# Merge stage of a hybrid attention and mixture-of-experts layer: order of work, early loads, logits from x1, and loads of the first stick-breaking head by columns

## The reference

```
h = rms_norm(x, g1); proj = h @ w_in
ya = banded attention of 8 heads;  yb = stick-breaking attention of 8 heads
gate = sigmoid(gates + b_gate)
merged = gate[0] * (ya @ w_proj_a) + gate[1] * (yb @ w_proj_b)
x = x + merged @ w_out
h2 = rms_norm(x, g2)
x = x + moe(h2)      # top group of 4, top 2 of 8 experts in it, by logits h2 @ [w_group, w_router]
```

## Time and profile before

| what | value |
|---|---|
| three plain runs | 2718.91, 2720.12 (median), 2724.43 us |
| profiled execution, its own time | 2722.95 us |
| its span, first to last instruction | 2721.1 us |
| PE busy, share of the span | 2603.6 us, 96% |
| DVE, ACT, POOL busy | 1634.5, 1491.1, 603.7 us |
| mean granted TensorE clock | 0.976 |
| stick-breaking stage | about 522 to 1290 us |
| merge stage | about 1290 to 1725 us |
| expert stage | about 1726 us to the end |

### The profile page before, as it was taken

One profiled execution on the slowest core, in us unless ns is written; L12 is line 12 of the kernel. 1 busy time (PEld: TensorE's weight loads), 2 busy tenths in 40 slices (PEclk: granted clock), 3 DMA queues, 4 the chain that ended last, 5 costly groups with the idle time before them and its releaser, 6 DMA issues. The chain is left out here.

```text
span 2721.1 us, 41174 instructions
## 1 busy us (share of the span) xinstructions
PE 2603.6 (96%) x13541; PEld 2154.9 (79%) x13542; DVE 1634.5 (60%) x2208; ACT 1491.1 (55%) x2641; POOL 603.7 (22%) x706
## 2 busy tenths in 40 slices
PE   7999999899999999999899999489999999999997
PEld 6788777678888888887799999477788888888886
DVE  4400555388777777776633433588766677766673
ACT  4312776477766676666321211368665577666563
POOL 0000111045444444443000000022211122212111
PEclk9999999999999999999799999699999999999999
DMA  5454444586566556632744433389866788866683
GB/s 174 133 198 150 124 132 129 158 288 211 189 205 190 175 168 188 205 125 99 235 126 132 132 118 96 149 313 390 316 224 228 241 281 313 314 232 223 222 299 64
DMA packets 196351, 536.65 MB, mean 197 GB/s; under 512 B 19928, under 2 KB 70552, under 8 KB 191744
## 3 DMA queue, kind: packets, MB, share of 16 engines
q1 hardware_dynamic: 169616, 432.80, 46.3%
q0 software_dynamic: 26608, 102.17, 13.7%
HBM read 403.36 MB, written 131.53 MB: 197 GB/s over the span
## 5 line engine op out<-in xcount | busy, mean ns | idle before, releaser
L1076 POOL TENSOR_TENSOR sb_sig<-sb_sig,sb_R 128x512 f32<-128x512 f32 (+1 forms) x320 | 340.9, 1065 | 412.9 <-DVE sb_R L1017 412.8
L51 PE MATMUL ex_ps_h<-ex_wu_hi,ex_x_hi 128*128 128x512 f32 x816 | 323.6, 397 | 2.4 <-DVE ex_x_lo L1837 2.4
L53 PE MATMUL ex_ps_h<-ex_wu_hi,ex_x_lo 128*128 128x512 f32 x816 | 319.5, 392 | 0.0
L52 PE MATMUL ex_ps_h<-ex_wu_lo,ex_x_hi 128*128 128x512 f32 x816 | 318.1, 390 | 0.0
L1842 DVE TENSOR_TENSOR ex_wu_lo<-ex_w,ex_wu_hi 128x1024 fp32r<-128x1024 f32 x248 | 285.3, 1217 | 2.5 <-ACT ex_wu_hi L1698 2.0
L1017 DVE TENSOR_TENSOR_SCAN sb_R<-sb_z,sb_R,sb_zeros 128x512 f32<-128x512 f32 x192 | 245.6, 1279 | 56.8 <-ACT sb_z L945 56.4
L1847 DVE TENSOR_TENSOR ex_wd_lo<-ex_w,ex_wd_hi 128x1024 fp32r<-128x1024 f32 x200 | 239.5, 1219 | 52.7 <-ACT ex_wd_hi L1705 52.6
L1698 ACT CAST ex_wu_hi<-ex_w 128x1024 fp32r<-128x1024 f32 x248 | 241.2, 1056 | 11.7 <-DMA ex_w<-in_w_exp 11.7
L957 ACT CAST sb_aT_hi<-sb_pst 128x512 fp32r<-128x512 f32 (+1 forms) x320 | 168.4, 526 | 136.3 <-PE sb_pst L1104 132.9
L1025 DVE TENSOR_TENSOR sb_aT_lo<-sb_pst,sb_aT_hi 128x512 fp32r<-128x512 f32 (+1 forms) x320 | 192.2, 601 | 53.7 <-ACT sb_aT_hi L957 51.0
L944 ACT ACTIVATE sb_sig<-sb_z 128x512 f32<-128x512 f32 (+1 forms) x320 | 172.4, 539 | 82.3 <-PE sb_z L1097 80.9
(11 more groups left out here) (274 smaller groups left out, 6256.5 us busy)
## 6 DMA issues: line engine op xcount, KB each, us to landing
ex_w<-in_w_exp SPq DMA_DIRECT2D x384, 512.0 KB, 8.9
sb_w_hi<-wg_d SPq DMA_DIRECT2D x48, 512.0 KB, 3.6
sb_w_lo<-wg_d SPq DMA_DIRECT2D x48, 512.0 KB, 4.6
gates<-sb_go SPq DMA_DIRECT2D x64, 256.0 KB, 3.8
mo_gates<-gates SPq DMA_DIRECT2D x64, 256.0 KB, 3.7
h<-mo_rows POOLq DMA_DIRECT2D x17, 512.0 KB, 3.0
nt_x<-in_x SPq DMA_DIRECT2D x16, 512.0 KB, 4.6
vhl<-nt_vo SPq DMA_DIRECT2D x16, 512.0 KB, 5.6
```

What stands on the lines that cost most here:

```text
L51: nc.tensor.matmul(out, w_hi, x_hi, start=first, stop=False)
L52: nc.tensor.matmul(out, w_hi, x_lo, start=False, stop=False)
L53: return nc.tensor.matmul(out, w_lo, x_hi, start=False, stop=last)
L1076: nc.gpsimd.tensor_tensor(sig[:, j % 5, 0:width], sig[:, j % 5, 0:width], R[:, r, first:first + width], ALU.mult).then_inc(a_done, 1)
```

## The change

In the stick-breaking stage the first head is loaded in four parts of 512 columns, each with a semaphore of its own, and other loads stand between them; the bias load goes to the end of this list. `round_w` and `split_w` of a piece are placed at step 2 + pc + 2 it at the earliest. In place of the second `wp` tile, SP loads the first chunk of `yaT` into slot 1 of `stage`.

```diff
             load_head(0, slice(0, TC))
-            sp.dma_start(bias[:, :], b_gate).then_inc(bias_in, 16)
-            load_head(0, slice(TC, S))
             load_w(2)
             keep_w(0)
+            load_head(0, slice(TC, 2 * TC))
+            load_w(3)
+            load_head(0, slice(2 * TC, 3 * TC))
             load_v(0)
-            load_w(3)
             keep_w(1)
+            load_head(0, slice(3 * TC, S))
+            sp.dma_start(bias[:, :], b_gate).then_inc(bias_in, 16)
...
-                    for n in range(2):
-                        sp.dma_start(w[:, n, :, :], wp_tiles[n, :, :, :]).then_inc(wp_in[n], 16)
+                    sp.dma_start(w[:, 0, :, :], wp_tiles[0, :, :, :]).then_inc(first_in_next[0], 16)
+                    sp.dma_start(w[:, 1, :, :].rearrange("p k c -> p (k c)").rearrange("p (t s) -> p t s", t=4),
+                                 yaT[:, :, 0:2 * P].rearrange("t p s -> p t s")).then_inc(first_in_next[1], 16)
...
-                        if j == pair_end(it, 2 * pc + 1) + 1:
+                        if j == max(pair_end(it, 2 * pc + 1) + 1, 2 + pc + 2 * it):
                             round_w(it + 2, pc)
...
-                if j % UH == 0 and h or j == 4:
-                    pe.wait_ge(head_in[u], (h // 2 + 1) * 96)
+                if h == g == r == 0:
+                    pe.wait_ge(first_in[ch], 96)
+                if j % UH == 0 and h:
+                    pe.wait_ge(head_in[u], (h + 1) // 2 * 96)
```

```diff
+    AHEAD = NO + 4
+    READ = [range(n + 2, n + 3) for n in range(NO - 2)] + [range(0), range(NO, NO + 1)]
+    READ += [range(n + 1, n + 2) for n in range(NO, AHEAD)]
+    LATE = range(AHEAD + 1, NW)
...
+    def units_after(n):
+        return range(min(AHEAD + 4 * n, NU), min(AHEAD + 4 * n + 4, NU))
...
+            act.wait_ge(early_in[0], 16)
+            nc.scalar.copy(wp_hi[:, 0, 0:KD // 2, :], w0[:, 0:KD // 2, :]).then_inc(early_rounded, 1)
+            act.wait_ge(early_in[1], 16)
+            nc.scalar.copy(y_hi[:, 0, 0:2, :], y_source(0, 0)[:, 0:2, :]).then_inc(early_rounded, 1)
+            nc.scalar.copy(y_hi[:, 0, 2:4, :], y_source(0, 0)[:, 2:4, :]).then_inc(y_rounded, 1)
+            nc.scalar.copy(wp_hi[:, 0, KD // 2:KD, :], w0[:, KD // 2:KD, :]).then_inc(w_rounded, 1)
             round_y(0, 1)
             round_w(1)
+            nc.scalar.preload_act_table(ACT.Sqrt)
+            for n in range(AHEAD):
+                if n == NO:
+                    round_y(1, 0)
+                    round_y(1, 1)
+                for i in READ[n]:
                     round_w(i)
                 round_m(n)
+            for i in LATE:
                 round_w(i)
...
+            for n in range(NT):
+                norm(n)
+                take_x1T(n)
+                for u in units_after(n):
+                    round_m(u)
+                if n % 2 == 0 and n // 2 + 2 < NCH:
+                    round_y(n // 2 + 2, 0)
+                    round_y(n // 2 + 2, 1)
...
+                nc.vector.scalar_tensor_tensor(logits[:, n, :], ps_l[:, 0:NR], rstd[:, n % 2:n % 2 + 1], b_bc[:, :],
+                                               ALU.mult, ALU.add).then_inc(l_read, 1)
...
+            def quarter(n, hf, q):
+                if hf == q == 0:
+                    pe.wait_ge(x1_done, n)
+                    if n % 2 == 0:
+                        pe.wait_ge(m_split, (n // 2 + 1) * NO)
+                slices(n, hf, range(q * KD // 2, (q + 1) * KD // 2))
...
+            for u in range(AHEAD):
                 unit(u)
+            for k in range(KD):
+                pe.wait_ge(m_split, k + 1)
+                pe.wait_ge(w_split, NO + k + 1)
+                for hf in range(2):
+                    slices(0, hf, (k,))
...
+            for n in range(NT):
+                behind = units_after(n)
+                if len(behind):
+                    unit(behind[0])
+                    turn(n)
+                    unit(behind[1])
+                    route(n)
+                    unit(behind[2])
+                    unit(behind[3])
+                if n + 1 < NT:
+                    quarter(n + 1, 0, 0)
+                    if not len(behind):
+                        turn(n)
+                    quarter(n + 1, 0, 1)
+                    if not len(behind):
+                        route(n)
+                    quarter(n + 1, 1, 0)
+                    quarter(n + 1, 1, 1)
+            turn(NT - 1)
             route(NT - 1)
```

More of the change, by code:

```diff
@@ L749, in stick_breaking_and_gates @@
 def stick_breaking_and_gates(nc, qk_hi, qk_lo, vhl, h0_hi, h0_lo, hT_d, w, w_in, wg_tiles, wg_d, b_gate, ident_d, neg_ident, mask_d,
[L750 removed]
+                             ybT, gates, wp_tiles, yaT, first_in_next, old_sems, ya_stored, stored, g_stored):
     QUADS = [(h, g, ch) for h in range(HB) for g in range(NC_) for ch in range(g, NC_)]
@@ L819, in stick_breaking_and_gates @@
         const_in, prep, zeros_set = sem("sb_const_in"), sem("sb_prep"), sem("sb_zeros_set")
-        bias_in, first_in = sem("sb_bias_in"), sem("sb_first_in")
+        bias_in, first_in = sem("sb_bias_in"), [sem(f"sb_first_in{ch}") for ch in range(NC_)]
         head_in, v_in = [sem("sb_head_in0"), sem("sb_head_in1")], [sem("sb_v_in0"), sem("sb_v_in1")]
@@ L1179, in merge_and_output_projection @@
         y_hi, y_lo = sb("mo_y_hi", [P, 2, 4, CT], F32R), sb("mo_y_lo", [P, 2, 4, CT], F32R)
-        last_slot = sb("mo_rows", [P, D])
-        rows = [stage[:, 0, :, :].rearrange("p k c -> p (k c)"), stage[:, 1, :, :].rearrange("p k c -> p (k c)"),
-                last_slot[:, :]]
+        third_slot = sb("mo_rows", [P, D])
+        flat = [stage[:, v, :, :].rearrange("p k c -> p (k c)") for v in range(2)]
+        rows = [flat[0], third_slot[:, :], flat[1]]
         y = sb("mo_y", [P, 4, CT])
@@ L1287, in _ @@
             pool.wait_ge(x1_stored, NT * 16)
-            pool.wait_ge(h2_stored, NT * 16 + 32)
         @block.scalar
         def _(act):
-            nc.scalar.preload_act_table(ACT.Sqrt)
             def round_w(i):
@@ L1402, in _ @@
             split_y(0, 1)
             split_w(1)
-            for n in range(NO):
-                for i in range(READ[n], READ[n + 1]):
+            for n in range(AHEAD):
+                if n == NO:
+                    split_m(NO - 1)
+                    split_y(1, 0)
+                    split_y(1, 1)
+                for i in READ[n]:
                     split_w(i)
                 weigh(n)
-                if n:
+                if n and n != NO:
                     split_m(n - 1)
-            split_m(NO - 1)
@@ L1411, in _ @@
[L1411 removed]
+            split_m(AHEAD - 1)
+            for i in LATE:
                 split_w(i)
[L1413 to L1431 removed]
@@ L1432, in _ @@
-            take_logits(NT - 1)
+            dve.wait_ge(const_in, 64)
+            nc.vector.tensor_tensor(wr[:, :, :], wr[:, :, :], g2T[:, :].unsqueeze(2).to_broadcast([P, KD, NR]),
+                                    ALU.mult).then_inc(wr_ready, 1)
+            for n in range(NT):
+                norm(n)
+                for i, u in enumerate(units_after(n)):
+                    weigh(u)
+                    if i:
+                        split_m(u - 1)
+                    if i == 2:
+                        take_logits(n)
+                if len(units_after(n)):
+                    split_m(units_after(n)[-1])
+                else:
+                    take_logits(n)
+                if n % 2 == 0 and n // 2 + 2 < NCH:
+                    split_y(n // 2 + 2, 0)
+                    split_y(n // 2 + 2, 1)
@@ L1508, with routing_and_experts @@
 BT = MAXB + 3
-def routing_and_experts(nc, logits, cst, h2_d, w_pieces, ident_d, out, stage):
+def routing_and_experts(nc, logits, cst, h2_d, h2_stored, w_pieces, ident_d, out, stage):
     with ExitStack() as c:
@@ L1998, in build @@
         merge_and_output_projection(nc, yaT, ybT, gates, wp, wo, x, g2, wr, ident, h2, out, logits, cst_d, cst, b_all, b_bc,
-                                    stage, mo_w_in, yb_stored, gates_stored)
-        routing_and_experts(nc, logits, cst, h2, w_exp, ident, out, stage)
+                                    stage, mo_w_in, g2T, h2_stored, yb_stored, gates_stored)
+        routing_and_experts(nc, logits, cst, h2, h2_stored, w_exp, ident, out, stage)
 def constants():
```

237 lines of the change are left out of this document (104 added, 133 removed).

## The result

The changed kernel takes 2731.33 us (median of 5 runs, 2728.6 to 2734.4); the kernel before, on the same chip, 2721.62 us. The ratio is 1.0034, 95% interval 1.0022 to 1.0045: slower by 6 to 12 us. The forecast was 2720, its range ended at 2728. The profiled execution has a span of 2726.8 us (2721.1 before); the two differ also in stages that the diff doesn't touch, so I compare stage by stage.

| profiled execution | stick-breaking | merge | logits to experts | all else | span |
|---|---|---|---|---|---|
| before | 763.9 | 437.7 | 43.9 | 1475.5 | 2721.1 |
| after | 773.5 | 435.3 | 47.2 | 1470.8 | 2726.8 |

What follows compares the result with a forecast made beforehand. The prediction took TensorE (PE), busy 96% of the span, as the bound. Its terms, +6.8 - 9.8 + 2.9 = -0.1 us, took the profiled 2722.95 to 2722.9; with the median 2.8 us lower, 2720 us, range 2713 to 2728.

Steps and rivals of the forecast that it cites:

- part 1: Start of stick-breaking: the rounding wait goes, but the late bias holds ACT, then PE; +6.8 us, bounds +6.0 and +9.5.
- part 2: Start of the merge stage: PE starts 5 us earlier, unit 12 comes sooner; -9.8 us, bounds -12 and -6.
- part 3: Merge stage's steady part and end: same work in another order, with some new stalls; +2.9 us, bounds 0 and +6.
- I take 0.8 us: Stick-breaking's loads: extra time for head 0's column pieces with 2 KB rows, putting the bias landing at 552.8.
- bound of 2.8: Stick-breaking's loads: extra us if the 2.3 MB behind the first column moved at 175 instead of 224 GB/s.
- the ring's start: Merge stage: the first weigh of the DVE and ACT piece cycle at 1299.5, piece 2 having landed by 1297.3.
- the gates: Merge stage: weigh(6) comes 0.65 us later if its gates, issued after split_m(3), take the usual 4.2 us.
- POOL loads the first x once 14 pieces are split: +0.6: Merge stage's steady part: POOL's load of the first x after 14 split pieces costs 0.6 us.
- B: Stick-breaking: the 8 KB bias is not held back, PE resumes at 548.4, part 1 is 0; 2713 us, chance 0.13.
- C: Merge stage wins more: clock stays up after unit 8's wait, stalls hidden; -12 and +1, 2716 us, chance 0.17.
- D: Stick-breaking: 128 KB column pieces are slow, 8 us a column instead of 3.5, bias later; 2733 us, chance 0.18.
- A: The main forecast: in stick-breaking one held transfer merely replaces another; own range 2716 to 2725 us, chance 0.52.

Runs made afterwards that it cites:

- e1: The changed kernel with the bias load moved back to right behind the first column of head 0; 2722.7 us, ratio 1.0007.
- e2: The kernel before with only the bias load moved to the end of the first list of loads; 2727.9 us, ratio 1.0025.
- m3: e3 with SyncE waiting for x(0) to land before it issues cst and the loads that follow; 2716.1 us, ratio 0.9983.
- e3: The changed kernel with stick-breaking's head 0 loads, bias load and rounding steps as before, leaving the merge stage's change alone; 2719.5 us, ratio 0.9997.
- c1: e4 with the merge-stage edits of m2 and m3 added; 2710.6 us, ratio 0.9963.
- m1: e3 with the two loads of y(1) issued behind weight pieces 4 and 5 instead of 8 and 9; 2719.8 us, ratio 0.9993.
- m2: m1 with both roundings and splits of y(1) moved ahead of piece 8 and weigh(7); 2717.6 us, ratio 0.9983.
- e4: The changed kernel with the bias load second and the other three columns of head 0 loaded in one piece; 2719.8 us, ratio 0.9992.
- c2: e3 with the edits of m2 and m3, stick-breaking as in the kernel before; 2712.9 us, ratio 0.9969.

## Why the prediction was wrong, step by step

| term | forecast | measured |
|---|---|---|
| part 1, until PE resumes | +6.8 | +8.8 |
| stick-breaking's rest | 0 | +0.8 |
| part 2, until unit 12 | -9.8 | -7.7 |
| part 3, the rest of the stage | +2.9 | +5.3 |
| sum | -0.1 | +7.2 |

(Part 1: from the first gate matmul to scores(4), 24.85 us before, 33.68 after. Part 2: unit 12 stands 66.8 us behind stick-breaking's last matmul; the forecast's place for it in the kernel before was 74.5. Part 3: what is left of the stage's -2.4.) The four terms add up to 7.2 of the 9.7 us between the medians. The rest isn't placed; the way from the logits to the experts may hold 1 us of it. So the forecast missed by 2.0, 2.1 and 2.4 us in its three parts, by 0.8 in stick-breaking's rest, and by what isn't placed.

- **Part 1, the mechanism: right.** The bias lands last, ACT is held at the first gate sigmoid, everything behind it too. e1 and e2 show it from both sides: 8.6 us less and 6.8 us more. From that sigmoid to scores(4) it took 2.58 us, forecast 2.5.
- **Part 1, the size: the step that failed is "I take 0.8 us" for the columns.** The forecast counted from the landing of the last store in the kernel before, 28.4 us behind the first gate matmul. The bias landed at 31.1: the columns' term is **2.7 us**, which gives 1.9 of the 2.0 us that part 1 missed by. (Against e2 it is 3.4; the same transfers landed 0.9 us sooner in e2 than in the kernel before, so that is how far one profile tells.) 2.7 us is the size of the bound of 2.8 that I had worked out from 175 GB/s. I had explained that rate of the earlier trace rows away by the slice's DMA share of 0.93. But a share near 1 doesn't tell the rate: 1.00 stands beside 240 GB/s in e2, 1.05 beside 394 in after. And I had put nothing down for the end of the queue, where the share fell to 0.35.
- **Part 2, the start: right.** First matmul 4.5 us behind stick-breaking's end (forecast 4.6), waits of 0.57 at four units (forecast 0.8 at three), a turn of 3.71 us, the half clock behind unit 8, `wo` never waited for.
- **Part 2, the ring's start and the gates: two terms too small.** Weigh(0) came 13.3 us behind the stage's border instead of 12.0: piece 2 shares its buffer with the first y and could be issued only after that was split, at 1298.35. Weigh(6) waited 1.92 us instead of 0.65. I had given these gates the median landing of the earlier trace rows, but the new order puts 1 MB into the queue just before them. Together that is unit 8 at +42.9 instead of +40.1; 0.8 of it was given back at half clock by unit 12.
- **Part 3, "POOL loads the first x once 14 pieces are split: +0.6": the term that was most wrong.** I counted when x is issued and not what it meets. It took 8.7 us to land, PE waited 2.86 us for x1(0) and then lost 1.5 us at 0.50 (by the comparison in m3): 4.4 us instead of 0.6. In e3 taking this collision away was worth 3.4 us of the median and 5.2 us of the stage up to the last route, more than all that the merge stage had won. The other terms hold, two stalls of 1.32 us (forecast 1.4), 1.32 and 1.32 us at the end; in sum they came out 1.4 us lower than forecast, and no run says where.
- **The rivals.** B fell: the small transfer does land behind the large ones. C fell: the clock went down. D named the term, slow column pieces, at 4.5 us a column; it was 0.9 to 1.1 us, below the 1.7 from which I had let it decide. That the time, 2731, lies next to D's 2733 is luck: it took the terms of the merge stage as well. By the sign for part 1 (the first gate sigmoid, before 547 for B, after 556 for D; in the kernel before's times it came at 554.7) A holds. My own sign of failure, a merge stage that shrinks by less than 3 us, is what happened (2.4; 0.8 to 4.6 in the five kernels with the same code).

What the failures share: a transfer was priced by how long one like it took before, and not by what is in the queues at its new place. The three merge edits were expected to give 10.4 us over e3's merge stage, and c1 gives 8.9: waits for loads (m1, m3), the place of two roundings in ACT's and DVE's order (m2), and the half clock behind both. No engine has less work.

## What to carry to other kernels

When an order of loads is changed, list what each waiting instruction's load now stands behind, on its own queue and on the other one, and add up the bytes; a small load that a busy engine waits for goes first. Splitting a load so that its first part arrives sooner shortened the wait for that part here (5.84 to 1.26 us) and cost more than this elsewhere in the same queue: e4, with the load whole, was 2.9 us faster than e1. And if all transfers of a stretch are needed within it, moving the instructions that wait for them moves the wait.

## What the hardware did that I had not expected

- An 8 KB transfer took 18.0 and 10.1 us to land behind full queues, 5.4 us behind the first column: it lands when its neighbours do, 0.16 us behind the last of them in e2. Yet SP's queue isn't strictly in order. In the kernel before, its transfers of this stretch landed in the order of issue; in after, a column piece of 128 KB issued at 529.35 landed at 537.4, and the 512 KB of gate weights issued ahead of it, at 528.73, at 539.8. Both in one window of after (count, KB, us to landing):

```profile
w_stage<-in_w_gate SPq DMA_DIRECT2D x1, 512.0 KB, 11.1
sb_q<-qk_hi SPq DMA_DIRECT2D x1, 128.0 KB, 8.1
```

- 64-partition pieces of 128 KB with 2 KB rows moved at 134 to 186 GB/s at a DMA share of 0.81 to 0.86, the same bytes in pieces of 384 KB with 6 KB rows at 240 to 267 GB/s. Other transfers were in these slices too, and where the third column moved beside gate weights, 536 to 540 in after, there were 219 and 279 GB/s; so this is no price of the row length. The Trainium skill gives a 64-partition transfer half of the ports and an asymptote of about 218 GB/s (SBUF — State Buffer, Door 1). The 6 KB rows in e2, with almost nothing else landing, lie somewhat above it; the last column of after, with little else beside it, far below, at 119 and 95 GB/s and a share of 0.73 and 0.35.
- PE's clock stayed at 1.00 (2.4 GHz) behind unit 8's gap of 2.65 us in c1 and was 0.50 (1.2 GHz) behind those of 2.61 us in m2 and 2.74 in c2, with the same matmuls before it (c1 waited 0.57 us once less among them). At x1(0) it stayed up behind 1.97 us and fell behind 2.86 to 4.09. The length of such a gap alone doesn't tell which. It is one profile of each.
